# Neighbourhood values projected token by token before the head pairs, kept in DRAM and fetched per pair

## The reference, cut to what matters

```python
def na_layer(a, mem_k, mem_v, w_in, w_out, rpb):
    proj = a @ w_in                                   # 1024 -> q | k | v (768 each) | memory query (256)
    q, k, v, mq = jnp.split(proj, [TOK_WIDTH, 2 * TOK_WIDTH, 3 * TOK_WIDTH], axis=-1)
    o = neighbourhood_attention(to_heads(q, 12), to_heads(k, 12), to_heads(v, 12), rpb)
    m = memory_attention(mq, mem_k, mem_v)            # 4 heads into 256 memory tokens
    return jnp.concatenate([from_heads(o), m], axis=-1) @ w_out
# neighbourhood_attention: grid of 16 rows x 64 columns; a query sees 8 rows x 16 columns of keys,
# softmax(q k / 8 + relative bias) @ v, with the keys' and values' rows shifted at the edges
```

## Time and profile before

| | us |
|---|---|
| median of three runs (lowest, highest) | 2343.06 (2342.62, 2343.98) |
| the profiled execution's own time | 2344.97 |
| its span in the trace | 2343.2 |
| PE busy | 2274.2 (97%) |
| DVE, ACT, POOL busy | 1213.2 (52%), 908.4 (39%), 1068.0 (46%) |
| mean granted PE clock | 0.995 |

### The profile page before, as it was taken

The page is one execution under the profiler, slowest core; times in us unless marked ns, Lnnn a source line. Parts: engine busy times, 40 slices in busy tenths (PEclk is TensorE's granted clock), DMA queues, the critical chain, the costliest instruction groups (busy, mean ns, idle before and its releaser), DMA issues.

```text
span 2343.2 us, 32221 instructions
## 1 busy us (share of the span) xinstructions
PE 2274.2 (97%) x12008; PEld 1846.1 (79%) x12008; DVE 1213.2 (52%) x2075; ACT 908.4 (39%) x1827; POOL 1068.0 (46%) x771
## 2 busy tenths in 40 slices
PE   7999999999999999999989999988999999999998
PEld 6788888887888888888877777766878888888886
DVE  4644444637644444676853333345476444447767
ACT  5521121455232332444644444444552332334443
POOL 4122222467988888100342222212789888880000
PEclk9999999999999999999999999999999999999999
DMA  5121111343443332833441111122424433338334
GB/s 211 46 83 52 48 53 46 126 153 109 143 149 104 104 112 96 315 103 99 163 110 46 49 49 49 50 98 91 184 90 149 141 107 108 95 108 328 95 99 153
DMA packets 115656, 264.25 MB, mean 113 GB/s; under 512 B 33183, under 2 KB 33454, under 8 KB 113454
## 3 DMA queue, kind: packets, MB, share of 16 engines
q1 hardware_dynamic: 115502, 262.20, 33.5%
HBM read 196.88 MB, written 65.30 MB: 112 GB/s over the span
## 4 chain that ended last, share of the span: by engine, by line
PE 88%; ACT 3%; DVE 2%; POOL 2%; issue 1%; DMA 0%; SPq 0%; DVEq 0%; POOLq 0%; ACTq 0%
PE PS L2050 26%; PE PS L2052 26%; PE PS L2051 26%; PE PS L2312 2%; PE PS L2542 2%; PE PS L2527 2%; PE PS L2412 1%; PE PS L2494 1%; PE PS L2337 1%; PE PS L2400 1%; PE PS L2300 1%; PE PS L2424 0%; PE PS L2425 0%; PE PS L2423 0%; DMA stage<-in_wpack 0%
## 5 line engine op out<-in xcount | busy, mean ns | idle before, releaser
L2050 PE MATMUL PS<-AOP,OPS 128*128 128x512 f32 x1216 | 473.9, 390 | 5.1 <-DVE AOP L1599 3.2
L2052 PE MATMUL PS<-AOP,OPS 128*128 128x512 f32 x1216 | 473.2, 389 | 0.0
L2051 PE MATMUL PS<-AOP,OPS 128*128 128x512 f32 x1216 | 473.1, 389 | 0.0
L756 POOL TENSOR_TENSOR wlo<-stage,whi 128x1024 fp32r<-128x1024 f32 x82 | 200.2, 2447 | 486.9 <-ACT whi L982 486.7
L2050 PE MATMUL PS<-aT,whi 128*128 128x512 f32 (+1 forms) x768 | 314.0, 409 | 10.8 <-ACT Vc L1447 4.8
L2052 PE MATMUL PS<-aT,wlo 128*128 128x512 f32 (+1 forms) x768 | 299.2, 390 | 0.0
L2051 PE MATMUL PS<-aT,whi 128*128 128x512 f32 (+1 forms) x768 | 298.3, 388 | 0.0
L809 POOL TENSOR_TENSOR OPS<-TW,OPS 128x512 fp32r<-128x512 f32 x176 | 261.1, 1497 | 77.4 <-ACT OPS L1068 77.4
L2050 PEld LDWEIGHTS PS<-AOP,OPS 128*128 128x128 f32 x1216 | 228.2, 188 | 54.6 <-POOL OPS L809 4.0
L2051 PEld LDWEIGHTS PS<-AOP,OPS 128*128 128x128 f32 x1216 | 228.3, 188 | 47.3
L2052 PEld LDWEIGHTS PS<-AOP,OPS 128*128 128x128 f32 x1216 | 228.2, 188 | 47.3
(11 more groups left out here) (211 smaller groups left out, 3882.5 us busy)
## 6 DMA issues: line engine op xcount, KB each, us to landing
stage<-in_w SPq DMA_DIRECT2D x100, 512.0 KB, 3.8
stage<-in_wpack SPq DMA_DIRECT2D x82, 512.0 KB, 3.3
hidden_scratch<-HT SPq DMA_DIRECT2D x154, 256.0 KB, 2.2
SRAW<-hidden_scratch SPq DMA_DIRECT2D x154, 256.0 KB, 2.7
BW<-in_w SPq DMA_DIRECT2D x16, 1024.0 KB, 8.0
h_scratch<-Hb SPq DMA_DIRECT2D x24, 512.0 KB, 3.6
Hb<-h_scratch SPq DMA_DIRECT2D x24, 512.0 KB, 5.4
cat_scratch<-OC SPq DMA_DIRECT2D x14, 512.0 KB, 4.9
```

Of the source, the lines that this page charges most:

```text
L756: pool.tensor_tensor(wlo[:, slot, :], stage[:, slot, :], whi[:, slot, :].bitcast(F32), ALU.subtract)\
L2050: pe.matmul(dst, stat[0], mov[0], start=start, stop=False, skip_group_check=onto)
L2051: pe.matmul(dst, stat[0], mov[1], start=False, stop=False, skip_group_check=onto)
L2052: return pe.matmul(dst, stat[1], mov[0], start=False, stop=stop, skip_group_check=onto)
```

## The change

The values of all 12 heads are projected first, during memory attention, with tokens on partitions. The stationary operand is now a 128-token slice of `aT`, the moving one 384 columns of value weights (three head pairs). There are four passes s (column half s // 2, token half s % 2), each of four weight units u (two k each) by four token tiles i, six matmuls of 384 columns each (`value_tile`). ACT and DVE copy each finished tile to `Vs`; SP stores the two column windows to `value_scratch` in DRAM, and fetches `Vc` of a pair (12 DMAs, rows of 512 bytes) one to two pairs ahead, into one of two buffers. A value unit is 768 columns wide; twelve are loaded, since two of each pair of passes are used in both.

Memory attention is now filled with 64 value tiles and 17 pieces (query and key of pair 0, one of pair 1). `vTn`, its copies and the transposes are gone. The six pairs are one sequence T = 0 to 99 of row tiles; every T has one piece of filler (`filler`) up to T = 78, and from T = 81 the output projection. ACT's `take_q` and weight split stand at T % 8 = 6, DVE's `take_k` at T % 16 = 14.

```diff
+            def value_tile(s, u, i):
+                n, th = value_unit(s, u), s % 2
+                if i == 0:
+                    pe.wait_ge(w_lo, n + 1)
+                if u == 0:
+                    pe.wait_ge(*(EV[U_NA + i // 2] if s == 0 else ((v_ea, v_ed)[i % 2], 2 * s - 1 + i // 2)))
+                rows = slice(i * P, (i + 1) * P)
+                for a in range(2):
+                    k, cols = 2 * V_K[(n - U_V) % len(V_K)] + a, slice(VB * a, VB * a + VB)
+                    ins = three(PS[:, i, 0:VB], (aT[:, th, 0, k, rows], aT[:, th, 1, k, rows]),
+                                (whi[:, w_slot(n), cols], wlo[:, w_slot(n), cols]), u == 0 and a == 0, u == 3 and a == 1)
...
             def mem_step(run, t, fill=()):
-                for n, k in fill[:2]:
-                    project(n, k)
+                ahead = max(2, len(fill) // 2)
+                for item in fill[:ahead]:
+                    fill_in(item)
                 if 0 <= t - 2 < tiles:
                     turn_probs(r0 + t - 2)
...
-                for c in range(8):
-                    ins = turn_values(c, 4 + c // 4)
-                ins.then_inc(vn_tr, 1)
-                pe.wait_ge(pt_ev, r0)
-                pe.wait_ge(o_ev, o_count(r0))
-                for c in range(8, 16):
-                    ins = turn_values(c, 4 + c // 4)
-                ins.then_inc(vn_tr, 1)
-                pieces(hp, range(AHEAD, EARLY))
-                pe.wait_ge(vn_a, 2 * hp - 1)
-                for c in range(16, 24):
-                    ins = turn_values(c, c // 4)
...
+            def filler(T):
+                piece, t = T + 1, T - (HP - 1) * ROWS
+                if piece < (HP - 1) * ROWS:
+                    project(U_NAH + 2 + piece // KD, piece % KD)
+                if 0 < t < LAST:
+                    for m in range(24 * (t - 1) // (LAST - 1), 24 * t // (LAST - 1)):
+                        out_rows(1, 0, m // TT, range(m % TT, m % TT + 1), first_set_free(1))
+            for T in range(0, tiles + 4, 2):
+                if 0 <= T - 3 < tiles:
+                    turn_probs(R_ROW + T - 3)
+                filler(T)
+                if 0 <= T - 4 < tiles:
+                    pair_values(T - 4)
+                if T < tiles:
+                    pair_scores(T)
+                if 0 <= T - 2 < tiles:
+                    turn_probs(R_ROW + T - 2)
+                filler(T + 1)
...
+            def store_values(s):                       # SP
+                sp.wait_ge(v_ea, 2 * s + 2)
+                sp.wait_ge(v_ed, 2 * s + 2)
+                for w in range(2):
+                    for p in range(2):
...
+                        sp.dma_start(dst, Vs[at_p:at_p + KC, s % 2, :, :]).then_inc(v_st[s % 2], 16)
+            def load_values(hp):                       # SP
+                for b in range(2):
+                    sp.wait_ge(v_st[b], 64 if hp < HP // 2 else 128)
+                if hp >= 2:
+                    sp.wait_ge(oc_rdy, 10 + hp - 1)
...
+                        sp.dma_start(Vc[0:keys, hp % 2, first:first + 2 * n - 1:2, :], src).then_inc(vc_ld[hp % 2], 16)
...
+            for T in range(HP * ROWS + 4):             # ACT
+                if T < HP * ROWS:
+                    probs(R_ROW + T, False)
+                if 0 <= T - 2 < HP * ROWS:
+                    take_pt(R_ROW + T - 2)
+                t = T - (HP - 1) * ROWS
+                if t < 0 and T % KD == KD - 2:
+                    n = next_unit(T)
+                    if T % ROWS < KD:
+                        take_q(n, qpair[:, (T // ROWS + 1) % 2, :, :])
+                    his(n + RING + 1)
+                if t == 0:
                     cat_split(1, range(1))
```

392 lines of the change are left out of this document (199 added, 193 removed).

## The result

The changed kernel takes 2322.09 us (median of four runs, 2320.86 to 2323.73) against 2342.84 for the kernel before in the same measurement: ratio 0.9913, 95% interval 0.9901 to 0.9925. It is 20.8 us faster; 23.7 were predicted. The profiled execution took 2323.73 us, with a span of 2321.9 and a granted clock of 0.993.

The account below looks back on a forecast made before the run. It took PE, with work in 97% of the span, to bound the kernel. Gains and losses summed to 23.7 us, taking the median from 2343.06 to 2319.4 us, range 2311 to 2333 (forecast's own 2315 to 2324, chance 0.45).

Parts of the forecast that it names:

- Steps 1 and 2: Pair starts: PE's value transposes go, 17.6 us gained, and its waits for the copies into `Vc`, 4.8 us gained.
- Step 3: Value projection: 384 matmuls of 384 columns at 0.173 us each replace 288 of 512 columns, 1.2 us lost.
- Step 4: Memory attention: the wait for the first exponentials goes, 1.0 us gained; more entries into wide matmuls, 1.9 us lost.
- some 54 us longer: Sign in the profile after: memory attention would last this much longer than before.
- Step 5: Pair loop: joining pairs gains 2.5 us, POOL's weight splits holding normalisations lose 2.5; 42.8 us a pair before these collisions.
- Step 6: Going into the last pair: PE idle 4.6 us in place of 5.7, 1.1 us gained.
- Step 7: Going into the last pair: half of the 4.6 us lost to a slow clock comes back, 2.3 us gained.
- A: Pair loop without collisions, full clock into the last pair, extra entries hidden: 2312.7 us, chance 0.17.
- B: Value projection: value weights come late, ten units by 1.3 us each: 2332 us, chance 0.11.
- C: Pair loop: POOL's splits hold DVE's normalisations, each hit costing most of 2.1 us: 2338 us, chance 0.07.
- D: Turns T = 0 to 79: with less filler the softmax chain sets them at 5.86 us: 2343 us, chance 0.05.
- E: Pair starts: `Vc` from DRAM comes late, 4.5 us of waiting in each of five pairs: 2342 us, chance 0.05.

Follow-up runs that it names:

- Run 1: Kernel before, with pairs 2 to 6 reusing pair 1's `Vc`, so without their value transposes, copies and most waits for them: 2325.07 us, ratio 0.9929.
- run 3: Kernel after with each pair run to its end before the next, the three steps without filler spread over the pair: 2328.08 us, ratio 0.9940.
- run 6: Kernel after with POOL's weight split at a pair's end put ahead of the next pair's mask operations: 2320.65 us, ratio 0.9909.
- run 7: Kernel after with ACT's weight splits one tile later, behind that step's `PT` copy: 2320.90 us, ratio 0.9909.
- run 4: Kernel after with twelve unused 512-column matmuls added at tiles 79 and 80, going into the last pair: 2321.62 us, ratio 0.9916.
- run 8: Kernel after with two tiles of the concatenated heads fetched and split early and the output product started at step -1 of the last pair: 2314.33 us, ratio 0.9881.
- Run 2: Kernel after with each pair run to its end before the next, the three steps without filler standing together: 2343.56 us, ratio 1.0003.
- run 5: Kernel after without the fetches of `Vc` for pairs 3 to 6, which reuse those of pairs 1 and 2: 2322.07 us, ratio 0.9917.
- run 10: Combination of run 9 with the last pair's output row tiles two at each odd step, none at even ones: 2308.51 us, ratio 0.9860.
- run 9: Kernel after repeated: 2322.17 us; its combination, the kernel after with the edits of run 8, run 6 and only the query's split of run 7: 2310.40 us, ratio 0.9866.
- run 11: Kernel of run 10 with the third `catT` tile's split at step 3 of the last pair, not 2: 2305.37 us, ratio 0.9840.

## Why the prediction was right, and where its terms were off

The time fell inside the forecast's own range: 20.8 us were gained of the 23.7, most of it from the terms that made up most of the sum, the transposes and the wait behind them. The miss of 2.9 is +2.3, -0.8 and -4.4 in the first three stages below, so part of how near the total came is luck. By stage, in the two profiled executions (a gain is positive). The predicted column holds the prediction's terms where they lie, and the pieces that left a stage, at 0.682 us for three matmuls: 24 such threes left the first stage, 64 the second, 8 the third. So the first is -66.6 + 16.4 + 2.9 + 1.0 + 1.0 - 1.9, the second 43.6 + 4 x 3.88, the third 5.5 + 2.9 + 1.1 + 2.3.

| stage | before | after | measured | predicted |
|---|---|---|---|---|
| first memory scores to first pair's | 73.66 | 118.56 | -44.9 | -47.2 |
| tile 0 to tile 64 | 232.21 | 173.89 | +58.3 | +59.1 |
| tile 64 to tile 84 | 66.99 | 59.57 | +7.4 | +11.8 |
| tile 84 to the end | 38.56 | 38.55 | 0.0 | 0 |

- **Steps 1 and 2** (22.4): right in kind and about in size. Run 1 has 3.34 us for a start of a pair of which 3.88 were summed; in its total of 18.4 the last start, with gains of other steps in it, makes up for that.
- **Step 3** (-1.2): right to the third digit, 0.1733 us a turn.
- **Step 4** (+1.0, -1.9): the wait went, as forecast. The 1.9 for the entries did not show, and that is most of the +2.3 of the first row. An entry does cost something: behind transposes the first two value matmuls start 0.26 us apart (1221.36 and 1221.62), where 0.173 is the rule. But before, the four transposes stood right ahead of scores or values and took 0.53 us to the next start (1217.07 to 1217.60 in before); ahead of value matmuls they take 0.35 (1221.01 to 1221.36). By these rows the entries are moved and not added, which is my estimate of why they come to nothing. The sign "some 54 us longer" was off too, at 44.9: it took ten pieces out where twelve went, and left out the transposes and the wait (3.9) ahead of the first pair's scores.
- **Step 5**: the total of the loop is right to 0.8 us by luck. A pair in the row takes 44.06, where the sum has 43.3 and the sign said 42.5 to 43.5; the first, with its short first turn, takes 1.6 less than the sum's and makes up for most. Both terms were too small. The run-on is worth 2.07 a pair without the collision (45.34 in run 3, 43.27 in run 6) and 1.28 with it, not 0.5. The prediction got 0.5 by taking eight pieces' full time out of a pair that stands by itself; but without them its start and end are no longer covered. Run 1 has 54.70 with 24 pieces, so 43.8 would be left; run 3 has 45.34. The collision costs 0.79 a pair at the normalisation where 0.5 was taken, and the query's copy and the split behind it 0.44 (runs 6 and 7). With both away the period is 42.84, the 42.8 worked out from the earlier trace rows, though those had the query's wait in them.
- **Step 6** (+1.1): 4.47 us idle for the 4.6 forecast, and yet 0.3 gained between tiles 78 and 84 (6.18 us idle before, 5.84 after), since two more waits (0.62 and 0.74) stand in the two turns behind. Not the landing of `catf` was last but its place in ACT's row, behind the exponentials and `PT` of the same step. Step 6 also misread the wait of 3.19 in the earlier trace rows: the weight split that the row names ends at 1569.30, and PE goes on at 1569.95. What ended it was DVE's half of the `catT` split, held by that weight split like the normalisations:

```profile
1566.96 2.34 POOL L756 TENSOR_TENSOR wlo<-stage,whi 128x1024 fp32r<-128x1024 f32 x1 [7.79 <-ACT whi L982]
```
```profile
1567.44 2.42 DVE L1820 TENSOR_TENSOR catT<-catf,catT 128x512 fp32r<-128x512 f32 x1 [1.75 <-ACT catT L1290]
```

- **Step 7** (+2.3): wrong. The clock cost 28.21 x 0.18 = 5.1 before and 5.0 after (3.4 in the second profile of after). "One such stretch remains, so I take half" was a guess on a number; what counted is that the stretch that remains has both parts, waits of the softmax chain without filler, and then 2.2 us. With dummy work for the first part it cost 1.8 (run 4), with real work for both nothing (run 8). The Trainium skill ("TensorE: Matmul & The Clock Gate", HAM oscillation), by which waits between bursts of matmuls (for DMA, in its case) put the array back to half clock, would have had 0 for step 7, and the profiled execution agrees (5.1 and 5.0). The other starts of a pair, with waits of 0.66 and 0.51 us between full turns, kept 1.00.

In the row from tile 64 to 84, 4.4 are missing: 2.2 of step 7, 0.8 of step 6, 0.8 of the fifth pair's longer period; 0.6 is not accounted for.

**The rivals.** A (2312.7): of its three parts the hidden entries came true, the loop without collision and the full clock did not. B: no wait for a weight unit in memory attention, no idle time at all. C: the mechanism is real. Five of the ten splits held a normalisation, four of those made PE wait, for 0.66 to 0.69 us each and not 2.1. What spoke against it, that mask work made no such rows before, is not so: in before a normalisation of 1.33 us at 1401.05 ends 0.18 behind a mask operation on POOL. D: turns in the loop, but for the first, are 5.2 to 6.06, up to tile 78 on average 5.45 with the first (212.49 / 39). Run 2 shows the rival's mechanism where filler is missing in a row (pairs 47.35, the gain gone); with the gaps spread (run 3) two thirds of the gain are kept. E: none (run 5).

The wait of 1.56 us for `catT` at the end of the last pair (1.5 to 1.6 in the other versions, 1.9 in the last two) is the same collision once more, as read from the rows; no run removes it:

```profile
1593.56 2.39 POOL L827 TENSOR_TENSOR wlo<-stage,whi 128x1024 fp32r<-128x1024 f32 x1 [11.80 <-ACT whi L1057]
```
```profile
1594.07 2.42 DVE L1887 TENSOR_TENSOR catT<-catf,catT 128x512 fp32r<-128x512 f32 x1
```
```profile
1596.64 0.47 PE L2114 MATMUL PS<-whi,catT 128*128 128x512 f32 x1 [1.56 <-DVE catT L1887]
```

What stays open: what makes the clock fall behind a gap, and for how long. Tiles 78 to 84 took 20.97 and 20.13 us in two profiles of after, and 21.58 in runs 6 and 7, which ate part of their gain.

## What to carry to other kernels

Before filler is moved out of a loop, look at what it covers: at a loop's start and end the pipeline's own waits come up, and joining the loops is then part of the change and not an extra. An engine's row may have several places for filler; put it where a wait stands: here the same three matmuls cost their full 0.69 us in one place, and moving them to the other gave back 0.23 to 0.40. Where one engine's long instruction holds another (here a 2.4 us split on POOL and a normalisation on DVE), the order of two lines decides whether anyone waits. And compare the same turn of two profiles by its own instructions before a cause is named: in run 8 the turn that differs most has the same filler in both.

## What the runs showed of the hardware

- A matmul in fp32r costs 0.120, 0.1733 and 0.227 us at 256, 384 and 512 columns: at 2.4 GHz a column is 0.417 ns, so each has the same 0.013 us on top, whatever its width.
- A DVE normalisation with one tensor input, 0.39 us by itself, ends 0.17 to 0.19 us behind the POOL instruction that runs beside it: it took 1.84 us beside a 2.40 us split, and 1.59, 0.94 and 0.95 beside mask operations of 1.38, 0.79 and 1.38. What a hit costs is the rest of POOL's instruction. DVE's `catT` split, with two inputs, took 2.42 for 0.69. The instruction with scores from PSUM just ahead was not held (0.49 us at 1416.45, beside the split of 1416.32). The Trainium skill ("GPSIMD Engine Reference", Key points) names shared SBUF interfaces, with contention for DVE instructions in a 2-port mode or with two SBUF inputs; for the `catT` split the trace agrees, and in which mode the normalisation runs no run here shows.
- How the clock answers to short waits is not given by their sum. 1.13 and 1.13 us of idling in one turn were followed by a clock of 0.75 for 11 us in the profiled execution of run 10. In run 8, as in the combination of run 9, 0.62, 0.62, 0.43 and 1.14 stood at that place, with the row tiles of the output product between, and the clock stayed at 1.00. The three waits of 1.27, 1.01 and 1.32 in run 2 kept it at 1.00 three times and were followed by 0.76 the fourth time. So one profile can't show what such a wait costs; the executions of run 10 lie 5.4 us apart, those of run 11, where the turn has one wait of 0.47, 1.8.
